# First transpose of the triangular blocks, and the one behind the first merge level, moved from TensorE to VectorE in 32x32 blocks

## What is computed

```
lmat  = where(strict, einsum('bnhcd,bnhed->bnhce', kb, k) * decay, 0)     # kb = k * beta
a     = lmat + eye(C)
sol   = triangular_solve(a, concatenate([vb, kb*exp(g)], -1), lower=True, unit_diagonal=True)
...
def step(S, inp):                       # lax.scan over the chunks
    v_new = u_i - w_i @ S
    o = qg_i @ S + intra_i @ v_new
    S = S * gl_i + kd_i.T @ v_new
```

## Time and profile before

| | |
|---|---|
| median of 3 runs | 1116.32 us (1115.75 to 1116.85) |
| the profiled execution, its own time | 1114.29 us |
| its span, first to last instruction | 1112.3 us |
| mean granted TensorE clock | 0.989 |
| PE busy | 1063.9 us (96%) |
| DVE busy | 519.3 us (47%) |
| ACT busy | 308.6 us (28%) |
| POOL busy | 127.2 us (11%) |

### The profile page before, as it was taken

The page is one execution under the profiler, slowest core; times in us unless marked ns, Lnnn a source line. Parts: engine busy times, 40 slices in busy tenths (PEclk is TensorE's granted clock), DMA queues, the critical chain, the costliest instruction groups (busy, mean ns, idle before and its releaser), DMA issues.

```text
span 1112.3 us, 13434 instructions
## 1 busy us (share of the span) xinstructions
PE 1063.9 (96%) x5376; PEld 745.2 (67%) x5376; DVE 519.3 (47%) x1138; ACT 308.6 (28%) x763; POOL 127.2 (11%) x167
## 2 busy tenths in 40 slices
PE   5989999999999999999989999999999999999997
PEld 2445565565655657977989788788955665666786
DVE  5651224975965469576388204400038136453004
ACT  1170112101122356422201114311160366454112
POOL 4000000020300131100042104300000200010001
PEclk9999999998999999999999999999999999999999
DMA  8733544110222200100040222720221200000102
GB/s 255 264 114 114 165 138 152 38 39 1 76 88 75 76 1 1 39 1 1 1 152 15 82 76 80 244 76 29 75 76 52 76 1 0 1 1 1 38 1 95
DMA packets 68421, 78.08 MB, mean 70 GB/s; under 512 B 2699, under 2 KB 64134, under 8 KB 68359
## 3 DMA queue, kind: packets, MB, share of 16 engines
q1 hardware_dynamic: 64258, 68.96, 19.2%
q0 software_dynamic: 2432, 7.53, 2.0%
q10 hardware_dynamic: 1669, 0.72, 0.3%
HBM read 73.70 MB, written 3.51 MB: 69 GB/s over the span
## 4 chain that ended last, share of the span: by engine, by line
PE 84%; DVE 8%; ACT 4%; issue 1%; DMA 1%; POOL 1%; ACTq 0%; POOLq 0%; DVEq 0%
PE ps L1171 78%; PE ps L1324 4%; PE ps L1201 2%; DVE xreg L2149 1%; DVE phase L2157 1%; DMA wring<-in_mod_w 1%; ACT hT L861 1%; DVE xreg L2171 1%; ACT phase L1141 1%; DVE xreg L1878 0%; PE ps L1211 0%; DVE pad L2073 0%; DVE pad L2080 0%; POOL stat L628 0%; DVE phase L2294 0%
## 5 line engine op out<-in xcount | busy, mean ns | idle before, releaser
L1171 PE MATMUL ps<-hT,wring 128*128 128x512 f32 (+2 forms) x1376 | 364.7, 425 | 4.4 <-ACT hT L861 4.4
L1171 PEld LDWEIGHTS ps<-hT,wring 128*128 128x128 f32 x1376 | 205.1, 192 | 157.7 <-issue 153.1
L1171 PE MATMUL ps<-phase 128*128 128x512 f32 (+3 forms) x448 | 138.1, 448 | 10.8 <-DMA phase<-k_pos_p 4.0
L1171 PE MATMUL ps<-wring,mix 128*128 128x256 f32 x640 | 138.6, 379 | 3.5 <-issue 2.7
L1171 PEld LDWEIGHTS ps<-wring,mix 128*128 128x128 f32 x640 | 121.4, 190 | 20.3 <-issue 2.9
L1171 PEld LDWEIGHTS ps<-phase 128*128 128x128 f32 (+1 forms) x448 | 72.8, 195 | 62.4 <-issue 48.7
L1171 PE MATMUL ps<-wring,hT 128*128 128x256 f32 (+1 forms) x480 | 99.5, 370 | 0.0
L1171 PEld LDWEIGHTS ps<-wring,hT 128*128 128x128 f32 x480 | 89.0, 190 | 10.3
L2197 DVE SCALAR_TENSOR_TENSOR phase<-phase,yst 128x1024 f32<-128x1024 f32 x10 | 12.8, 1284 | 122.9 <-POOL yst L628 122.9
L1171 PE MATMUL ps<-xreg,phase 128*128 128x128 f32 (+1 forms) x416 | 53.7, 289 | 6.2 <-DVE xreg L2163 4.9
L1171 PEld LDWEIGHTS ps<-xreg,phase 128*128 128x128 f32 x416 | 48.2, 192 | 10.8 <-DVE xreg L2163 5.8
(11 more groups left out here) (313 smaller groups left out, 1232.9 us busy)
## 6 DMA issues: line engine op xcount, KB each, us to landing
wring<-in_mod_w SPq DMA_DIRECT2D x24, 1024.0 KB, 5.2
wring<-in_even_in_w SPq DMA_DIRECT2D x16, 1024.0 KB, 7.0
wring<-in_odd_in_w SPq DMA_DIRECT2D x9, 1024.0 KB, 5.2
wring<-in_even_out_w SPq DMA_DIRECT2D x4, 1024.0 KB, 7.0
wring<-in_odd_out_w SPq DMA_DIRECT2D x4, 1024.0 KB, 4.8
xreg<-in_x_sample SPq DMA_DIRECT2D x1, 2048.0 KB, 12.5
xreg<-in_x_sample POOLq DMA_DIRECT2D x1, 2048.0 KB, 8.0
out_y_sample<-xreg SPq DMA_DIRECT2D x4, 512.0 KB, 2.6
```

The lines of the kernel that those rows point to most:

```text
L1171: return nc.tensor.matmul(o, l, r, start=first, stop=last)
```

## The change

The first transposes of both groups (10 chains) and the ones behind the first merge level (10 chains) are no longer done by PE and copied by ACT. DVE does them with its own transpose, which transposes each 32x32 block of the array by itself, straight from `Uinv` to `Tinv` and back. The first ten are put into the loop of `invert_blocks`, one behind each multiplication; the others in `merge_level`, one behind each addition. PE now waits for these by two new semaphores, `T1_ready` and `U2_ready`. Before group 1's multiplications, DVE waits until `in_z0` is done on PE. The fillers ahead of group 1 go from five to nine; the banks of the removed transposes go out of the list.

```
-         ("inv0", CHAINS[0]), ("inv0_0", 3 * CHAINS[0]), ("keys2", 2), ("inv0_1", 3 * CHAINS[0]), ("keys3", 2),
+         ("inv0_0", 2 * CHAINS[0]), ("keys2", 2), ("inv0_1", 3 * CHAINS[0]), ("keys3", 2),
...
-         ("inv1", CHAINS[1]), ("inv1_0", 3 * CHAINS[1]), ("inv1_1", 3 * CHAINS[1]), ("inv1_2", 3 * CHAINS[1]),
+         ("inv1_0", 2 * CHAINS[1]), ("inv1_1", 3 * CHAINS[1]), ("inv1_2", 3 * CHAINS[1]),
...
@@ ACT @@
-                for m, (t, d) in enumerate(chains):
-                    f = g["T1"] + m
-                    wait_full(act, f)
-                    nc.scalar.activation(Tinv[t][:, d, :], bank(f), ACT.Copy).then_inc(free(f), 1)
-                for l in range(len(LEVELS)):
+                for l in range(1, len(LEVELS)):
...
@@ PE @@
-                keep_busy(g["T1"], 5 if g is inv_groups[1] else 3)
-                for n, (t, d) in enumerate(chains):
-                    pe.wait_ge(U1_ready, 2 * t + d + 1)
-                    turn4(g["T1"] + n, lambda h: Uinv[:, 2 * t + d, h * P:h * P + P])
+                keep_busy(g["levels"][0], 9 if g is inv_groups[1] else 3)
                 for l, b in enumerate(LEVELS):
                     fl = g["levels"][l]
                     for n, (t, d) in enumerate(chains):
-                        wait_drained(pe, g["T1"] + n if l == 0 else g["levels"][l - 1] + nch + n)
+                        if l == 0:
+                            pe.wait_ge(T1_ready, 2 * t + d + 1)
+                        else:
+                            wait_drained(pe, g["levels"][l - 1] + nch + n)
...
-                        if l > 0:
+                        if l == 1:
+                            pe.wait_ge(U2_ready, 2 * t + d + 1)
+                        elif l > 1:
                             wait_drained(pe, g["levels"][l - 1] + 2 * nch + n)
...
-                    for n, (t, d) in enumerate(chains):
+                    for n, (t, d) in enumerate(chains if l > 0 else ()):
                         wait_drained(pe, fl + nch + n)
                         turn4(fl + 2 * nch + n, lambda h: Tinv[t][:, d, h * P:h * P + P])
@@ DVE, invert_blocks @@
                 dve.wait_ge(dve_step, done[1])
+                if n == 1:
+                    wait_full(dve, start["in_z0"] + 2)
                 for i, t in enumerate(tiles):
                     for d in range(2):
                         tt(Uinv[:, 2 * t + d, :].rearrange("p (h k c) -> p h k c", h=H, c=BASE),
...
                            .broadcast_to([P, H, P // BASE, BASE]), ALU.mult).then_inc(U1_ready, 1)
+                        dve.wait_ge(U1_ready, 2 * t + d + 1)
+                        nc.vector.transpose(Tinv[t][:, d, :], Uinv[:, 2 * t + d, :]).then_inc(T1_ready, 1)
@@ DVE, merge_level @@
                     tt(Tv, Tv, bank(f)[:, 0:256].rearrange("p (h n b) -> p h n b", h=H, b=b), ALU.add)\
                         .then_inc(free(f), 1)
+                    if l == 0:
+                        wait_drained(dve, f)
+                        nc.vector.transpose(Uinv[:, 2 * t + d, :], Tinv[t][:, d, :]).then_inc(U2_ready, 1)
```

More of the change, by code:

```diff
@@ L137, in inverse_fills @@
     for n, tiles in enumerate(GROUPS):
-        groups.append({"tiles": tiles, "chains": [(t, d) for t in tiles for d in range(2)], "T1": start[f"inv{n}"],
-                       "levels": [start[f"inv{n}_{l}"] for l in range(len(LEVELS))]})
+        groups.append({"tiles": tiles, "chains": [(t, d) for t in tiles for d in range(2)], "levels": [start[f"inv{n}_{l}"] for l in range(len(LEVELS))]})
     return groups, sums, keys
@@ L411, in program @@
         U1_ready = sem("U1_ready")
+        T1_ready = sem("T1_ready")
+        U2_ready = sem("U2_ready")
         kd_ready = sem("kd_ready")
```

## The result

The changed kernel takes 1128.81 us (median of 4 runs, 1127.33 to 1130.01) against 1116.03 us (median of 4 runs of the kernel before): ratio 1.0117, interval 1.0098 to 1.0135. Forecast were 1110.3 us, with a range of 1108.8 to 1113.1. Its profiled execution took 1130.01 us, with a span of 1127.5 us.

What follows compares the result with a forecast made beforehand. PE was taken to bound group 0, DVE's inversion group 1's wait. Group 0's 3.0 us and the rest up to 3.4, plus 2.63 for second transposes, gave 6.0: 1116.32 - 6.0 = 1110.3 us, range 1108.8 to 1113.1.

Steps and rivals of the forecast that it cites:

- The granted clock is 1.00 in the stretch that holds this wait, so waits of this size do not lower it: In group 1 of the kernel before, PE's 1.41 us wait for DVE's line 2085 behind five fillers leaves the clock full.
- Clock 1.00 throughout: Expected profile of the changed kernel: PE's granted clock stays at 1.00 everywhere.
- rival 4: DVE transpose handles fp32 in two passes, 1.5 us each: slower, about 3.9 us more, 1120 us; 4 in 100.
- The chance of slower: Whole kernel: probability 0.05 given to a slower result, against 0.84 faster and 0.11 within about 0.2%.
- The price of the transpose: One DVE transpose of 512 columns, absent from the earlier trace: taken as 0.72 us, bounds 0.30 and 1.5 us.
- Rivals 1 to 4: Transposes ≤0.6 us: 1108.8 us (8 in 100); 0.80-1.1: 1111-1114 (12); about 1.24: 1116.0 (8); 1.5: 1120 (4).
- Group 0: Two rows of PE transposes go out; late `take_keys` and first level-two masking leave 3.0 us won, 0.5 less than both rows.
- The conflict with POOL: Group 0: POOL's masking delays the third and fourth multiplication, fourth transpose up to 2 us later, at 456.6, before 457.9.
- Group 1: First product ends 3.4 us sooner, set by DVE's sixth transpose; second transposes save 2.63 us; waits sum to 0.9 us.
- The four additional fillers: Ahead of group 1, nine in place of five: cost nothing for a transpose above about 0.57 us.
- Its state loads are issued when the last transpose is drained, so they shift with it: Scan behind the merge levels: its loads move along with the earlier end, scan at DVE's and PE's pace.
- Rival 5: Gain given back behind the scan, at a transfer that keeps its own time: no change; 3 in 100.

Runs made afterwards that it cites:

- e2: Kernel before, with only group 1's transposes behind the first merge level moved to DVE, five fillers, no added wait between products: 1114.53 us, ratio 0.9985.
- e4: Changed kernel with eleven fillers ahead of group 1 in place of nine: 1113.41 us, ratio 0.9975 to the kernel before.
- e6: Changed kernel with ten fillers ahead of group 1 in place of nine: 1113.27 us, ratio 0.9977 to the kernel before.
- e5: Changed kernel, nine fillers, with the first product of group 1's first level 128 columns a head, not 64: 1113.15 us, ratio 0.9975 to the kernel before.
- e3: Kernel before, with only group 1's first transposes moved to DVE behind nine fillers, waits kept: 1122.87 us, ratio 1.0058.
- e7: Changed kernel with five fillers ahead of group 1, as in the kernel before, in place of nine: 1130.21 us, ratio 1.0130 to the kernel before.
- e1: Kernel before, with only group 0's two sets of transposes moved to DVE; group 1 unchanged with five fillers: 1114.33 us, ratio 0.9980.
- e9: Kernel of e5 with the scan's two state loads issued early, when group 1's blocks are inverted: 1110.71 us, ratio 0.9949 to the kernel before.
- e10: Kernel before, with the two state loads issued early and nothing else: 1117.03 us, ratio 1.0008.
- e11: Changed kernel with the first product of group 1's second level 128 columns wide: 1119.77 us, ratio 1.0031 to the kernel before.

## Why the prediction was wrong

**The step that failed** is in its first part: "The granted clock is 1.00 in the stretch that holds this wait, so waits of this size do not lower it", and with it "Clock 1.00 throughout" at the end. That wait of 1.41 us stands between five products of 512 columns and transposes of 128 columns. I carried it over to three waits of 0.44 us that stand between products of 64 columns. The runs put the cases side by side. Narrow products without waits (e2, e4), narrow ones with one wait of 0.44 us (e6), and wide ones with all three (e5) keep the clock. Narrow ones with three waits lose it, be they 0.44 us each (the changed kernel, 16.4 us lost) or the first of them only 0.2 us (e3), and so do narrow ones behind a wait of 2.4 us (e7). What two waits do was not run. And the wait of 2.7 us behind the scan shows that no size of wait can be called safe from one profile: the same instructions kept the clock in three profiles and lowered it in ten. There was no rival for this; rival 4 had the sign, but for a price of the transpose that was not paid. The chance of slower, 0.05, was far too small for a change that takes the wide transposes out of the stretch and puts waits in.

The kernel before had shown the danger elsewhere, in a row that I had not asked for:

```profile
250.00:255.00 5.00, 5.00 (x26) 5.00 (x25) 0.00 (x0) 0.00 (x0) 0.00 (x0) 0.50 0.02 3
```

There PE is in the middle of 40 products of 16 columns (243 to 256 us), without an idle moment, and runs at the lower clock. A PE that is busy by the profile is no sign that its clock stays.

**The price of the transpose** was right: 0.72 us taken, 0.71 measured. The two groups of the changed kernel's DVE:

```profile
L2091 DVE STREAM_TRANSPOSE hT<-phase 128x512 f32<-128x512 f32 x6 | 4.3, 712 | 0.2
...
L2112 DVE STREAM_TRANSPOSE phase<-hT 128x512 f32<-128x512 f32 x6 | 4.3, 711 | 0.2
```

That is 1.39 ns a column with all fixed parts in it. The measurement lies nearer to "Vector Engine (DVE) Microarchitecture Reference" of the Trainium skill, section 3.8 (one element per cycle and lane), than to four times the 311 ns that "VectorE: DVE Perf Modes" of the Trainium skill, section on the three transpose paths, lists for 128x128 in bf16, an estimated 1.24 us. Rivals 1 to 4, which all hung on this price, are out.

**Group 0** came out as worked through: 3.0 forecast, 3.1 measured in e1, with `take_keys` as the next thing late. The conflict with POOL was there too:

```profile
453.97 1.28 DVE L2086 TENSOR_TENSOR phase<-pad,phase 128x512 f32<-128x512 f32 x1
455.28 0.71 DVE L2091 STREAM_TRANSPOSE phase<-phase 128x512 f32<-128x512 f32 x1
```

The third multiplication, with two SBUF inputs, took 1.28 us beside POOL and the fourth 1.02, not 0.69; the transposes stayed at 0.71. It stayed hidden behind the fillers, as said.

**Group 1** without the clock is right in its sum: DVE and not the fillers sets the end of the first product, and the forecast's 3.4 us up to that end (group 0's 3.0 in it) and 2.63 us for the second transposes are what e5 gives, 5.9 us in the stage against 6.0. But the waits were three, 1.3 us in all, and not two with 0.9, and that came mostly from a term that the forecast had mis-sized. It took 0.89 us a filler, from a length of five that holds the modelled end of the last; from start to start three take 2.57 us, 0.86 each, and the nine took 7.73 us (505.30 to 513.03) and not 8.03. So PE came to the fourth chain 0.3 us sooner than forecast and found its transpose not done. DVE's first multiplication, 5.3 us behind the end of `in_z0` and not 5.1, adds to it. The four additional fillers, which the forecast put at no cost and no use, were one too few to keep the clock (e6).

**What was to come behind the stage unchanged** did not quite. "Its state loads are issued when the last transpose is drained, so they shift with it" was right for their issue, but they landed 11.2 us behind it and not 9.9, over an edge that was 1.3 us away. e9 against e5 is 2.4 us by the medians, of which the scan's profile shows 1.35; the other 1 us is open. Rival 5, a gain given back at a transfer behind the scan's start, holds for this part. The larger part given back, an estimated 1.7 us, is the second fall of the clock behind the scan, and no rival had it. Open stays why the loads take longer: in both kernels they are issued among three weight chunks of 1 MB, the first of them 0.9 us ahead of the first load.

## What to carry to other kernels

When a change takes wide work (transposes, fillers) out of TensorE and puts a wait for another engine between narrow products, price the clock as a rival of its own: half speed until wide work comes again, here 16 us against 6 us won. Cover such waits, with a filler or by making the products in them wider where that costs no time; here 128 columns took as long as 64 (four products one each 0.89 us against 0.885, start to start) and kept the clock. Then look for falls of the clock outside the stretch that was changed, in every profile that is compared: the one behind the scan took 1.7 us of 6, and no instruction near it had been touched. After a win ahead of a load, look at how close behind the load its first use stood, and issue it as early as its memory is free; e10 says to measure that by itself, since there the median gained nothing.

## What was not expected of the hardware

- Three waits of 0.44 us, 1.3 us in all, among 64-column products brought the clock from 1.00 to 0.50 for 34 us, one did not (e6), and the same three among 128-column products did not (e5).
- At 0.50, 64-column products back to back for 30 us did not bring it back; with 128-column ones it was back after 4 to 5 us (transposes in the changed kernel and e3, the product in e11). "TensorE: Matmul & The Clock Gate" of the Trainium skill, part 1, says that the clock is held down by default and that activity releases it; the rise in e3 and e11 agrees, while the 30 us of 64-column products, which fill PE's row in the profile, did not release it here.
- Four fp32 products of 128 columns took 0.89 us from start to start (two chains in 1.78 us, 534.67 to 536.45 in e11), four of 64 columns 0.885 us; the 1.16 and 1.10 us in the timelines hold modelled ends.
- A wait of 2.7 us between fillers of 512 columns and products of 256 lowered the clock in ten of thirteen profiles, for an estimated 1.7 us (3.4 in e10), and left it at 1.00 in three.
